# A fused encoder block: the expert loop staged over two blocks, with paired weight rows and a plain fp32 down product

## Chip, cores and metric

One core of a Trainium2 chip. The metric is the device time of the whole kernel in microseconds, lower is better.

## What is computed

One encoder block on x of 1024 tokens by 1024 features, fp32, one sequence. First comes a convolutional mixer behind a norm and a conditioning (projections, two gated convolution branches, an output product). Then a second norm, and a mixture of experts: each token takes two of 32 SwiGLU experts. The tokens of an expert are gathered in blocks of 128 rows. Cut to what matters here:

```python
def expert_block(args):
    xblk, e = args                       # 128 x 1024
    a = xblk @ w_gate[e]                 # 1024 x 512
    u = xblk @ w_up[e]                   # 1024 x 512
    return (jax.nn.silu(a) * u) @ w_down[e]   # 512 x 1024

yb = lax.map(expert_block, (xb, blk_e)).reshape(n_rows, d)
yb = yb * w_buf[:, None]
out = jnp.zeros_like(xt).at[tok_buf].add(yb)
```

The result times a gate row (gt2) is added to x, and a last norm follows. With these inputs 33 blocks hold tokens; a block's empty rows are left out by the gather and the scatter.

## The kernel before

The code is one program with a list of instructions for each engine; order between engines is kept by semaphores, and every engine takes its own list strictly in order. The mixer (up to about 1040 us) and the routing (to about 1082 us) are not touched. There, as in the expert loop, a large product is made of three fp32r matmuls (`three`, lines 1162 to 1166): both operands are split into a high half (a cast, fp32r) and a low half (the operand less its high half), and hi x hi, hi x lo and lo x hi add up in PSUM. The statistics of the mixer (line 1220) use a plain fp32 matmul of the same shape, which the profile records as two.

**Buffers of the expert loop** (lines 214 to 225). A block's weights are six chunks of 128 x 2048 fp32, 1 MB each. Chunks 0 to 3 hold gate and up rows of four groups of 256 input features, chunks 4 and 5 the down rows. Each chunk exists once raw (`e_raw`), once high (`e_hi`) and once low (`e_lo`). The gathered rows `xg`, their transposed halves `xT_hi` and `xT_lo` and the output `y_sb` exist twice.

**SyncE** (lines 396 to 427) loads weights. For block b+1 it waits for each of the four gate/up chunks until VectorE has split block b's (`gu_lo`), issues two transfers of 512 KB (`load_gu`, L400), then for each down chunk until its split is done (`d_lo`), and issues one of 1 MB (`load_down`, L404).

**GpSimd** (lines 524 to 550) gathers the rows of block b+2 (L528) once TensorE has transposed those in that buffer, copies the indices and weights of block b, waits for ScalarE's output, multiplies it by the gate row (L545), scatters it with an add into DRAM (L547) and waits until that has landed.

**ScalarE** (lines 703 to 727), for each block: casts of down chunks 4 and 5 (L710), sigmoid of the first half of the gate columns (L712), cast of chunk 0 of the next block (L691), high half of the first transposed hidden rows (L715), sigmoid of the second half (L717), chunk 1, second hidden half (L720), chunk 2, high half of the next rows (L699), chunk 3, and the output out of PSUM times its weight (L727).

**VectorE** (lines 1129 to 1145) takes the same order for the low halves: L1135 for down chunks, L1104 for gate/up chunks, L1120 for hidden rows, L1108 for rows; L1114 and L1116 multiply gate and up.

**TensorE** (lines 1380 to 1401), for each block: gate/up of the first 256 hidden columns with all eight feature tiles, then of the other 256, down products of chunk 4, transposes of the hidden rows (L1343) and of the next block's rows (L1338), down products of chunk 5. Gate/up of the two halves are 48 matmuls of 512 columns, down 24. Chunk q is free for the next cast when the second half has used it (`gu_used`).

Names and lines that recur: `three` L1164 to L1166, `gate_up` L1346, `down` L1368, `gu_split` on ScalarE L687 and on VectorE L1102, `held` (a wait, L334), `f_o` L1154 in the final norm.

## Time and profile before

| | |
|---|---|
| device time, median of 3 runs | 1873.6 us (1873.36 to 1873.72) |
| span of the profiled execution | 1872.6 us |
| its mean granted TensorE clock | 0.947 |
| TensorE busy, whole kernel | 1619.8 us, 86% |
| VectorE busy | 1380.1 us, 74% |
| ScalarE busy | 808.7 us, 43% |
| GpSimd busy | 359.5 us, 19% |
| packets of SyncE's queue, share of 16 engines | 47.5% |

The page gives a span, from the first to the last instruction, and no separate time for the profiled execution; the median of the runs is 1.0 us above that span. A row of a group of instructions has the line, engine, operation, tiles written and read, shapes and count, then busy us and mean ns of one, then idle time of the engine before them and what ended it. Matmuls overlap, so the mean of one is longer than the distance between starts.

### The profile page before, as it was taken

What the parts mean: (1) busy time and instruction counts of PE and PEld (TensorE: products, weight loads), DVE (VectorE), ACT (ScalarE), POOL (GpSimd) and SP (SyncE); (2) the same over time, 40 slices, a digit from 0 to 9 for tenths busy, and PEclk for the clock granted to TensorE, in tenths of its full rate; (3) what the DMA queues carried; (4) which work ended last, traced back from release to release, by engine and by line L of the source; (5) the groups of instructions that cost most, each with busy time, mean ns of one, the idle gap of its engine ahead of it and who ended that gap; (6) DMA issues with size and microseconds to landing.
All of it is one profiled execution on the core that took longest, in us unless ns stands there. A gap on an engine that the chain in (4) does not pass through costs nothing.

```text
span 1872.6 us, 21983 instructions
## 1 busy us (share of the span) xinstructions
PE 1619.8 (86%) x7040; PEld 1306.4 (70%) x7040; DVE 1380.1 (74%) x1217; ACT 808.7 (43%) x738; POOL 359.5 (19%) x274
## 2 busy tenths in 40 slices
PE   2799999999999979979899568888888888888880
PEld 2688888888888857757688456666666666666660
DVE  5686977868769783483454568888888888888885
ACT  3411111111021122142221257777777777777773
POOL 0100000000000000000000034344444444333441
PEclk9999999999999989989999679999999999999995
DMA  7422313323233244233352468988888888998845
GB/s 259 127 90 86 116 56 123 101 90 106 73 100 113 67 153 143 74 117 119 121 175 90 169 223 308 304 306 307 306 302 304 300 308 307 311 319 304 308 142 193
DMA packets 201362, 352.05 MB, mean 188 GB/s; under 512 B 17228, under 2 KB 90956, under 8 KB 201333
## 3 DMA queue, kind: packets, MB, share of 16 engines
q1 hardware_dynamic: 184630, 309.71, 47.5%
q0 software_dynamic: 16704, 41.98, 7.7%
q8 instruction: 16, 0.26, 0.1%
q14 instruction: 12, 0.10, 0.0%
HBM read 323.84 MB, written 46.66 MB: 198 GB/s over the span
## 4 chain that ended last, share of the span: by engine, by line
PE 48%; DMA 18%; POOL 12%; issue 12%; DVE 7%; ACT 1%; POOLq 1%; SPq 0%; DVEq 0%; ACTq 0%
DMA d_x<-y_sb,s_idx 17%; PE ps L1164 15%; PE ps L1165 15%; PE ps L1166 15%; POOL xg L528 5%; POOL y_sb L545 4%; POOL g_idx L526 2%; PE ps L1220 1%; DVE macc L797 1%; PE ps L1286 1%; POOL s_idx L540 1%; DVE f_o L1154 1%; DVE s L912 1%; DVE conf L903 0%; DMA prow<-in_c_dram 0%
## 5 line engine op out<-in xcount | busy, mean ns | idle before, releaser
L1164 PE MATMUL ps<-A_hi,w_hi 128*128 128x512 f32 x1024 | 402.5, 393 | 23.5 <-DVE A_lo L892 13.0
L1165 PE MATMUL ps<-A_lo,w_hi 128*128 128x512 f32 x1024 | 400.7, 391 | 0.0
L1166 PE MATMUL ps<-A_hi,w_lo 128*128 128x512 f32 x1024 | 400.6, 391 | 0.0
L1104 DVE TENSOR_TENSOR e_lo<-e_raw,e_hi 128x2048 fp32r<-128x2048 f32 x136 | 380.4, 2818 | 1.1 <-issue 1.1
L882 DVE SCALAR_TENSOR_TENSOR conv_acc_b<-glu,colc,conv_acc_b 128x1024 f32<-128x1024 f32 x232 | 298.0, 1285 | 10.5 <-DVE rows L874 1.4
L691 ACT CAST e_hi<-e_raw 128x2048 fp32r<-128x2048 f32 x136 | 259.4, 1910 | 51.5 <-PE ps L1166 51.5
L1164 PE MATMUL ps<-e_hi,xT_hi 128*128 128x512 f32 x528 | 224.8, 426 | 62.1 <-DVE e_lo L1104 59.7
L1164 PEld LDWEIGHTS ps<-A_hi,w_hi 128*128 128x128 f32 x1024 | 193.8, 189 | 65.9 <-issue 17.8
L1165 PEld LDWEIGHTS ps<-A_lo,w_hi 128*128 128x128 f32 x1024 | 193.9, 189 | 40.6 <-issue 0.5
L1166 PEld LDWEIGHTS ps<-A_hi,w_lo 128*128 128x128 f32 x1024 | 193.7, 189 | 40.6
L1165 PE MATMUL ps<-e_lo,xT_hi 128*128 128x512 f32 x528 | 218.1, 413 | 0.0
L1166 PE MATMUL ps<-e_hi,xT_lo 128*128 128x512 f32 x528 | 218.0, 413 | 0.0
L1164 PEld LDWEIGHTS ps<-e_hi,xT_hi 128*128 128x128 f32 x528 | 106.1, 201 | 97.8 <-DVE e_lo L1104 73.2
L1135 DVE TENSOR_TENSOR e_lo<-e_raw,e_hi 128x2048 fp32r<-128x2048 f32 x66 | 147.9, 2279 | 0.0
L577 ACT CAST w_hi<-w_raw 128x1024 fp32r<-128x1024 f32 x72 | 73.6, 1047 | 166.5 <-PE ps L1166 163.4
L1164 PE MATMUL ps<-e_hi,hT_hi 128*128 128x512 f32 x264 | 107.7, 408 | 38.5 <-DVE hT_lo L1120 38.5
L767 DVE TENSOR_TENSOR w_lo<-w_raw,w_hi 128x1024 fp32r<-128x1024 f32 x72 | 88.0, 1223 | 63.0 <-ACT w_hi L577 60.0
L1166 PEld LDWEIGHTS ps<-e_hi,xT_lo 128*128 128x128 f32 x528 | 106.3, 201 | 24.5
L710 ACT CAST e_hi<-e_raw 128x2048 fp32r<-128x2048 f32 x66 | 122.3, 1901 | 0.4
L1165 PEld LDWEIGHTS ps<-e_lo,xT_hi 128*128 128x128 f32 x528 | 106.6, 202 | 21.6
L545 POOL TENSOR_TENSOR y_sb<-y_sb,rows 128x1024 f32<-128x1024 f32 x33 | 82.7, 2507 | 125.2 <-ACT y_sb L727 125.2
L1166 PE MATMUL ps<-e_hi,hT_lo 128*128 128x512 f32 x264 | 104.4, 395 | 0.0
(227 smaller groups left out, 2140.4 us busy)
## 6 DMA issues: line engine op xcount, KB each, us to landing
e_raw<-in_w_gate_dram SPq DMA_DIRECT2D x132, 512.0 KB, 3.8
e_raw<-in_w_up_dram SPq DMA_DIRECT2D x132, 512.0 KB, 4.9
e_raw<-in_w_down_dram SPq DMA_DIRECT2D x66, 1024.0 KB, 8.4
w_raw<-in_w_in_dram SPq DMA_DIRECT2D x56, 512.0 KB, 4.2
stream<-in_w_ada_dram SPq DMA_DIRECT2D x48, 512.0 KB, 5.5
xn<-in_x_dram SPq DMA_DIRECT2D x8, 512.0 KB, 7.2
d_short<-conv_acc_a POOLq DMA_DIRECT2D x8, 512.0 KB, 4.0
d_gate_a<-gate_st POOLq DMA_DIRECT2D x8, 512.0 KB, 2.9
```

Of the source, the lines that this page charges most:

```text
L528: g.indirect_dma_start(xg[:, slot, :], None, d_h2, bass.IndirectOffsetOnAxis(ap=g_idx[:, slot:slot + 1], axis=0), bounds_check=S - 1, oob_ ...
L545: g.tensor_tensor(y_sb[:, s, :], y_sb[:, s, :], rows[:, GT2, :], ALU.mult).then_inc(s_yw, 1)
L577: a.copy(w_hi[:, slot, :], w_raw[:, slot, :]).then_inc(w_hi_done, 1)
L691: a.copy(e_hi[:, q, :], e_raw[:, q, :]).then_inc(gu_hi, 1)
L710: a.copy(e_hi[:, 4 + q, :], e_raw[:, 4 + q, :]).then_inc(d_hi, 1)
L767: v.tensor_tensor(w_lo[:, slot, :], w_raw[:, slot, :], w_hi[:, slot, :].bitcast(F32), ALU.subtract).then_inc(w_lo_done, 1)
L882: lstep(v.scalar_tensor_tensor(conv_acc_b[:], glu[:, t:t + S], w, conv_acc_b[:], ALU.mult, ALU.add))
L1104: v.tensor_tensor(e_lo[:, q, :], e_raw[:, q, :], e_hi[:, q, :].bitcast(F32), ALU.subtract).then_inc(gu_lo, 1)
L1135: v.tensor_tensor(e_lo[:, 4 + q, :], e_raw[:, 4 + q, :], e_hi[:, 4 + q, :].bitcast(F32), ALU.subtract).then_inc(d_lo, 1)
L1164: t.matmul(dst, st_hi, mv_hi, start=first, stop=False)
L1165: t.matmul(dst, st_hi, mv_lo, start=False, stop=False)
L1166: return t.matmul(dst, st_lo, mv_hi, start=False, stop=last)
```

## The change

A block's work is spread over two steps. Step b (lines with `b, par = pair * 2 + (1 + s), 1 - s`) does gate/up of block b and the down product of block b-1; block 0's gate/up stands ahead of the loop and the last down product behind it.

- Gate and up of a block go to one PSUM slot of their own, slots 0 and 1 in turn, and are done in one pass over the chunks. Slot 2 takes row transposes, slot 3 hidden transposes and the down product.
- `load_gu` gives a partition two consecutive rows (4 KB in one piece, before two pieces of 2 KB); the rows' transposes take every second column to match.
- The down product is one plain fp32 matmul in place of three, on raw weights and on hidden rows that are copied once and not split. Splits of chunks 4 and 5 and of the hidden rows go.
- A down chunk's buffer is free when TensorE has used it (`d_used`). SyncE loads gate/up of block b+2 and then down of block b+1.
- The SwiGLU part has one sigmoid and two multiplies of 512 columns.
- VectorE takes the output out of PSUM, times weight and gate row in one instruction; ScalarE's output copy and GpSimd's multiply go. GpSimd scatters it in the next step. The last block has buffers and index of its own.
- One sigmoid of one column is placed ahead of the loop on ScalarE.

```diff
             def load_gu(q, e):
                 for part, w in ((0, w_gate), (1, w_up)):
-                    dst = e_raw[:, q, :].rearrange("p (k w n) -> p k w n", k=2, w=2)[:, :, part, :]
-                    src = w[bass.ds(e, 1), 2 * q * P:2 * (q + 1) * P, :].rearrange("a (k p) n -> p (a k) n", p=P)
+                    dst = e_raw[:, q, part * D:(part + 1) * D].rearrange("p (k n) -> p k n", k=2)
+                    src = w[bass.ds(e, 1), 2 * q * P:2 * (q + 1) * P, :].rearrange("a (p k) n -> p (a k) n", p=P)
                     sp.dma_start(dst, src).then_inc(e_full[q], 16)
...
             with sp.Fori(0, NBLK) as b:
-                with sp.If(b < n_blk):
-                    with sp.If(b + 1 < n_blk):
-                        e_next = sp.value_load(tab[0:1, bass.ds(b + 1, 1)], min_val=0, max_val=NE - 1)
+                with sp.If(b + 1 < n_blk):
+                    with sp.If(b + 2 < n_blk):
+                        e_gu = expert_of(b + 2)
                         for q in range(4):
-                            held(gu_lo, b * 4 + (q + 1))
-                            load_gu(q, e_next)
-                        for q in range(2):
-                            held(d_lo, b * 2 + (q + 1 + CREDIT_DOWN))
-                            load_down(q, e_next)
-
-                    with sp.If(n_blk < b + 2):
+                            held(gu_lo, b * 4 + (4 + q + 1))
+                            load_gu(q, e_gu)
+                    with sp.If(n_blk < b + 3):
                         for q in range(4):
-                            sp.wait_ge(gu_lo, b * 4 + (q + 1))
+                            sp.wait_ge(gu_lo, b * 4 + (4 + q + 1))
                             sp.sem_inc(e_full[q], 32)
+                    e_down = expert_of(b + 1)
+                    for q in range(2):
+                        held(d_used, b * 2 + (q + 1))
+                        load_down(q, e_down)
...
+                        held(t_done, b + 1)
+                        gather(s, b + 2, b * 2 + 2)
+                        g.tensor_copy(s_idx[:, 1 - s:2 - s], idx_all[:, bass.ds(b - 1, 1)]).then_inc(p_copy, 1)
+                        held(p_copy, b * 2 + 3)
+
+                        pool.wait_ge(y_st, b * 16 - 16)
                         pool.sem_inc(y_free, 1)
+                        held(y_ev, b + CREDIT_Y)
+                        scatter(y_sb[:, 1 - s, :], s_idx[:, 1 - s:2 - s])
...
+            def h_hi(value):
+                act.wait_ge(ht_ps, value)
+                a.copy(hT[:].rearrange("p f n -> p (f n)"), ps[:, 3, 0:F]).then_inc(ht_sb, 1)
...
+            def gate(par, value, before):
+
+                act.wait_ge(gu_used, value)
+                if before is not None:
+                    act.wait_ge(a_h, before)
+                a.activation(sg[:], ps[:, par, 0:F], ACT.Sigmoid).then_inc(sgd, 1)
...
+            for q in range(3):
+                gu_split(q, 64, q + 1)
+            gate(0, 4, None)
+            gu_split(3, 64, 4)
             with act.Fori(0, NBLK // 2) as pair:
                 for s in range(2):
-                    with act.If(pair * 2 + s < n_blk):
-                        b = pair * 2 + s
+                    b, par = pair * 2 + (1 + s), 1 - s
+                    with act.If(b < n_blk):
+                        x_hi(1 - par, b + 2)
                         for q in range(2):
-                            act.wait_ge(e_full[4 + q], b * 16 + 16)
-                            act.wait_ge(d_used, b * 2 + (q - 1 + CREDIT_DOWN))
-                            a.copy(e_hi[:, 4 + q, :], e_raw[:, 4 + q, :]).then_inc(d_hi, 1)
-                        act.wait_ge(gu0, b + 1)
-                        a.activation(sg[:, 0, :], ps[:, 0, 0:F // 2], ACT.Sigmoid).then_inc(sgd, 1)
-                        gu_split(0, b * 32 + 64, b * 4 + 1)
-                        act.wait_ge(ht_ps, b * 2 + 1)
-                        a.copy(hT_hi[:, 0:2, :], ps[:, 3, 0:2 * P]).then_inc(ht_hi, 1)
-                        act.wait_ge(gu_used, b * 4 + 4)
-                        a.activation(sg[:, 1, :], ps[:, 0, F:F + F // 2], ACT.Sigmoid).then_inc(sgd, 1)
-                        gu_split(1, b * 32 + 64, b * 4 + 2)
-                        act.wait_ge(ht_ps, b * 2 + 2)
-                        a.copy(hT_hi[:, 2:4, :], ps[:, 3, 4 * P:6 * P]).then_inc(ht_hi, 1)
+                            gu_split(q, b * 32 + 64, b * 4 + (q + 1))
+                        h_hi(b)
                         gu_split(2, b * 32 + 64, b * 4 + 3)
-                        x_hi(1 - s, b + 3)
+                        gate(par, b * 4 + 4, b)
                         gu_split(3, b * 32 + 64, b * 4 + 4)
-                        act.wait_ge(d_used, b * 2 + (2 + CREDIT_DOWN))
-                        act.wait_ge(y_free, b + (CREDIT_STORE - 1))
-                        act.wait_ge(s_w, b + 1)
-                        a.activation(y_sb[:, s, :], ps[:, 2, :], ACT.Copy, scale=w_blk[:, s:s + 1]).then_inc(y_ev, 1)
+            h_hi(n_blk)
...
+            def hidden(par, n):
+
+                dve.wait_ge(sgd, n)
+                v.tensor_tensor(hid[:], ps[:, par, 0:F], sg[:], ALU.mult).then_inc(a_h, 1)
+                dve.wait_ge(a_h, n)
+                v.tensor_tensor(hid[:], ps[:, par, F:2 * F], hid[:], ALU.mult).then_inc(hd, 1)
+
+            def y_out(dst, blk, used):
+
+                dve.wait_ge(d_used, used)
+                v.scalar_tensor_tensor(dst, ps[:, 3, :], w_all[:, bass.ds(blk, 1)], rows[:, GT2, :], ALU.mult, ALU.mult).then_inc(y_ev, 1)
...
+            x_lo(1, 2)
+            for q in range(3):
+                gu_split(q, 4 + q + 1)
+            hidden(0, 1)
+            gu_split(3, 8)
             with dve.Fori(0, NBLK // 2) as pair:
                 for s in range(2):
-                    with dve.If(pair * 2 + s < n_blk):
-                        b = pair * 2 + s
+                    b, par = pair * 2 + (1 + s), 1 - s
+                    with dve.If(b < n_blk):
+                        x_lo(1 - par, b + 2)
                         for q in range(2):
-                            dve.wait_ge(d_hi, b * 2 + (q + 1))
-                            v.tensor_tensor(e_lo[:, 4 + q, :], e_raw[:, 4 + q, :], e_hi[:, 4 + q, :].bitcast(F32),
-                                            ALU.subtract).then_inc(d_lo, 1)
-                        hidden(0, b * 2 + 1, b * 2 + 1, hd0)
-                        h_lo(0, b * 2 + 1)
-                        gu_split(0, b * 4 + 5)
-                        hidden(1, b * 2 + 2, b * 2 + 2, hd1)
-                        gu_split(1, b * 4 + 6)
-                        h_lo(1, b * 2 + 2)
-                        x_lo(1 - s, b + 2)
+                            gu_split(q, b * 4 + (4 + q + 1))
                         gu_split(2, b * 4 + 7)
+                        hidden(par, b + 1)
                         gu_split(3, b * 4 + 8)
+                        dve.wait_ge(y_free, b)
+                        y_out(y_sb[:, 1 - par, :], b - 1, b * 2)
+            y_out(y_last[:], n_blk - 1, n_blk * 2)
...
             def rows_transpose(slot):
                 for k in range(KT):
-                    last = t.transpose(ps[:, 1, k * P:(k + 1) * P], xg[:, slot, k * P:(k + 1) * P], ident[:])
+                    pair_k = xg[:, slot, k // 2 * 2 * P:(k // 2 + 1) * 2 * P].rearrange("t (p w) -> t w p", w=2)
+                    cols_k = pair_k[:, k % 2, :]
+                    last = t.transpose(ps[:, 2, k * P:(k + 1) * P], cols_k, ident[:])
                 last.then_inc(t_done, 1)
 
-            def hidden_transpose(half):
-                for f in range(2):
-                    last = t.transpose(ps[:, 3, half * 4 * P + f * P:half * 4 * P + (f + 1) * P], hid[:, half, f * P:(f + 1) * P], ident[:])
+            def hidden_transpose():
+                for f in range(FT):
...
+            def gate_up(q, par, b):
+
+                pe.wait_ge(gu_lo, b * 4 + (q + 1))
+                for kk in range(2):
+                    k = 2 * q + kk
+                    for part in range(2):
+                        mv = slice(part * D + kk * F, part * D + (kk + 1) * F)
+                        last = three(ps[:, par, part * F:(part + 1) * F], xT_hi[:, par, k * P:(k + 1) * P], xT_lo[:, par, k * P:(k + 1) * P],
+                                     e_hi[:, q, mv], e_lo[:, q, mv], k == 0, k == KT - 1)
+                last.then_inc(gu_used, 1)
+
+            def down(q, value):
+
+                pe.wait_ge(e_full[4 + q], value)
+                for kk in range(2):
+                    f = 2 * q + kk
+                    for h in range(2):
+                        ch_ = slice(kk * D + h * H, kk * D + (h + 1) * H)
+                        last = t.matmul(ps[:, 3, h * H:(h + 1) * H], hT[:, f, :], e_raw[:, 4 + q, ch_], start=(f == 0), stop=(f == FT - 1))
+                last.then_inc(d_used, 1)
+
+            n_blk = pe.value_load(tab[0:1, NBLK:NBLK + 1], min_val=PAIRS // P, max_val=NBLK - 1)
             pe.wait_ge(xg_full[0], 16)
             rows_transpose(0)
+
+            pe.wait_ge(xg_full[1], 16)
+            pe.wait_ge(xTlo, 1)
+            rows_transpose(1)
+            for q in range(4):
+                gate_up(q, 0, 0)
             with pe.Fori(0, NBLK // 2) as pair:
                 for s in range(2):
-                    with pe.If(pair * 2 + s < n_blk):
-                        b = pair * 2 + s
+                    b, par = pair * 2 + (1 + s), 1 - s
+                    with pe.If(b < n_blk):
+                        pe.wait_ge(xg_full[1 - par], pair * 16 + 32)
                         pe.wait_ge(xTlo, b + 1)
-                        pe.wait_ge(hd0, b + 1)
-                        gate_up(0, s, b)
-                        pe.wait_ge(hd1, b + 1)
-                        gate_up(1, s, b)
-                        pe.wait_ge(ht_lo, b * 2 + (1 + CREDIT_DOWN))
-                        pe.wait_ge(d_lo, b * 2 + (1 + CREDIT_DOWN))
-                        pe.wait_ge(y_ev, b + 1)
-                        down(0)
-                        down(1)
-                        pe.wait_ge(hd1, b + 2)
-                        hidden_transpose(1)
-                        pe.wait_ge(xg_full[1 - s], pair * 16 + 16 * (1 + s))
-                        rows_transpose(1 - s)
-                        pe.wait_ge(ht_lo, b * 2 + (2 + CREDIT_DOWN))
-                        pe.wait_ge(d_lo, b * 2 + (2 + CREDIT_DOWN))
-                        down(2)
-                        down(3)
+                        rows_transpose(1 - par)
+                        pe.wait_ge(hd, b - 1 + CREDIT_HID)
+                        for q in range(2):
+                            gate_up(q, par, b)
+                        pe.wait_ge(hd, b + CREDIT_HID)
+                        pe.wait_ge(y_ev, b - 1 + CREDIT_Y)
+                        hidden_transpose()
+                        for q in range(2, 4):
+                            gate_up(q, par, b)
+                        pe.wait_ge(ht_sb, b)
+                        for q in range(2):
+                            down(q, b * 16)
+            pe.wait_ge(hd, n_blk + CREDIT_HID)
+            pe.wait_ge(y_ev, n_blk + (CREDIT_Y - 1))
+            hidden_transpose()
+            pe.wait_ge(ht_sb, n_blk)
+            for q in range(2):
+                down(q, n_blk * 16)
```

## Rows read from the trace of the kernel before

**Rows 1.** Busy time by stretch, 1300 to 1400 us; columns as the first row says.

```profile
core 0: us, PE busy (x) PEld busy (x) DVE busy (x) ACT busy (x) POOL busy (x), PEclk, DMA share, GB/s
1300.00:1400.00 100.00, 87.93 (x384) 69.90 (x384) 83.81 (x61) 74.07 (x64) 40.06 (x27) 0.95 0.87 303
```

**Rows 2.** Who TensorE waited for, blocks 1 to 32 (us in total, times, longest).

```profile
PE ps L1164 <- DVE e_lo L1104: 59.7, 32, 1.9
PE ps L1164 <- DVE hT_lo L1120: 36.2, 31, 1.2
```

**Rows 3.** Instruction groups of sixteen blocks, 1396 to 1750 us, each shape apart.

```profile
L1104 DVE TENSOR_TENSOR e_lo<-e_raw,e_hi 128x2048 fp32r<-128x2048 f32 x64 | 180.1, 2835 | 0.0
L691 ACT CAST e_hi<-e_raw 128x2048 fp32r<-128x2048 f32 x64 | 122.3, 1911 | 24.4 <-PE ps L1166 24.4
...
L1135 DVE TENSOR_TENSOR e_lo<-e_raw,e_hi 128x2048 fp32r<-128x2048 f32 x32 | 71.7, 2279 | 0.0
...
L1108 DVE TENSOR_TENSOR xT_lo<-ps,xT_hi 128x1024 fp32r<-128x1024 f32 x16 | 19.6, 1225 | 18.8 <-ACT xT_hi L699 18.8
...
L699 ACT CAST xT_hi<-ps 128x1024 fp32r<-128x1024 f32 x16 | 16.3, 1018 | 0.0
...
L720 ACT CAST hT_hi<-ps 128x256 fp32r<-128x256 f32 x16 | 6.0, 374 | 13.3 <-PE ps L1343 13.3
```

**Rows 4.** Timeline of one block, TensorE: start us, us, engine, line, operation.

```profile
1404.50 0.39 PE L1164 MATMUL ps<-e_hi,xT_hi 128*128 128x512 f32 x1
...
1408.35 0.39 PE L1166 MATMUL ps<-e_hi,xT_lo 128*128 128x512 f32 x1
...
1420.85 1.04 PE L1338 MATMUL ps<-ident,xg 128*128 128x128 f32 x8
```

**Rows 5.** TensorE by shape: the plain fp32 matmul of the statistics, whole kernel.

```profile
L1220 PE MATMUL ps<-conf,mean_w 128*128 128x512 f32 x32 | 13.9, 592 | 0.0
```

**Rows 6.** Timeline of SyncE's transfer issues in one block.

```profile
1410.81 0.37 SPq L400 DMA_DIRECT2D e_raw<-in_w_gate_dram  x1
1411.28 0.42 SPq L400 DMA_DIRECT2D e_raw<-in_w_up_dram  x1
1412.94 2.56 SPq L404 DMA_DIRECT2D e_raw<-in_w_down_dram  x2
```

**Rows 7.** SyncE's load of an expert number (L416): duration, first and last start.

```profile
L416 SPq SEQ_ASSERT  x2: 18/18/18, 1417.0 to 1438.4; - x2
```

**Rows 8.** Transfers: down loads (L404) to landing; issue table of the page.

```profile
DMA to landing us min/median/max: 5.7/8.4/17.4
...
e_raw<-in_w_gate_dram SPq DMA_DIRECT2D x132, 512.0 KB, 3.8
e_raw<-in_w_up_dram SPq DMA_DIRECT2D x132, 512.0 KB, 4.9
```

**Rows 9.** Transfers in 1038 to 1040, 1050 to 1056 and 1398.94 to 1752.9 us.

```profile
DMA packets 416, 0.82 MB, mean 410 GB/s; under 512 B 16, under 2 KB 16, under 8 KB 416
...
DMA packets 859, 2.48 MB, mean 413 GB/s; under 512 B 55, under 2 KB 55, under 8 KB 858
...
DMA packets 47950, 109.00 MB, mean 308 GB/s; under 512 B 4961, under 2 KB 4961, under 8 KB 47950
...
q0 software_dynamic: 4608, 8.99, 10.5%
```

**Rows 10.** Timeline of the first block.

```profile
1088.26 1.97 PE L1338 MATMUL ps<-ident,xg 128*128 128x128 f32 x8 [8.84 <-DMA xg<-d_h,g_idx]
...
1092.67 0.79 PE L1164 MATMUL ps<-e_hi,xT_hi 128*128 128x512 f32 x1 [2.44 <-DVE xT_lo L1108]
...
1101.10 0.38 ACT L712 ACTIVATE sg<-ps 128x256 f32<-128x256 f32 x1 [3.51 <-PE ps L1166]
```

**Rows 11.** Timeline of the last block.

```profile
1827.92 1.11 ACT L727 ACTIVATE y_sb<-ps,w_blk 128x1024 f32<-128x1024 f32 x1 [0.20 <-PE ps L1166]
```

**Rows 12.** Chain that ended last, its end.

```profile
1832.46 5.77 DMA d_x<-y_sb,s_idx
```

134 lines of the change are left out of this document (56 added, 78 removed).

## The prediction

> **What bounds the kernel now.** I read the busy time by stretch first. In the expert loop, VectorE is busy 84 of 100 us, TensorE 88, the transfer engines 87 [rows 1]: nobody is full, so something alternates. The waits say what: in 32 blocks TensorE waits 59.7 us for L1104 (the low half of a gate/up chunk) and 36.2 us for L1120 (the low half of the hidden rows), 3.0 us a block [rows 2]. One block's splits can only begin when the block before has used its chunks, and its down product is too short a cover. The chain that ended last runs through GpSimd's scatters, but GpSimd sits idle before each and only its last scatter sets the end [rows 12]. Sixteen blocks take 354 us [rows 3], 22.1 each.
>
> **The change, part by part.** I call step i the time T(i) to T(i+1) in which TensorE transposes rows of block i+1, does gate/up of block i, and at the end the down product of block i-1. There are 33 blocks, steps 1 to 32, with block 0's gate/up ahead and the last down product behind.
>
> *TensorE.* Gate/up keeps 48 matmuls: 17 starts apart take 3.85 us, so 0.228 us each [rows 4], 10.95 us. The down product loses 24 matmuls of 0.23 (5.5 us) and gets 8 plain fp32 ones. The statistics show that kind: 16 in code, 32 in the profile, 13.9 us, 0.868 us each [rows 5], so 6.95 us, dearer by 1.4. Twelve transposes at 0.13 (eight in 1.04 [rows 4]) are 1.55, and hand-overs I put at 0.2. Sum **19.65 us** if nothing makes it wait; both old waits go, since a chunk's split now has a period less 2.7 us to be ready and costs 1.91 + 2.28 [rows 3]. Transposes with a stride of two words are not in the trace: nothing lost, or double, 1.0 us; I take nothing, as the columns are as many. It lies before the point that I find decisive below.
>
> *VectorE* loses two splits of 2.28, 4.6 us, and the low halves of the hidden rows. L1104 and L1135 are one shape with means of 2835 and 2279 ns [rows 3]; the difference lies in the split beside GpSimd's multiply, which goes too, 4 x 0.56 = 2.2 us. It gains the weighted output, near L1108's 1.23 (1024 columns out of PSUM), say 1.3. From about 18.6 (84% of 22.1) to 13 us a block: no bound. *ScalarE* loses two casts of 1.91 and the output copy; its new cast of 512 hidden columns lies between 0.37 (256) and 1.02 (1024) [rows 3], 0.6. The table load I price at nothing either way: it can run while ScalarE waits. *GpSimd* loses the multiply; its scatter now goes out about 2.5 us into the next step and its gather of two blocks ahead behind that, over ten us before it is needed, so that move costs nothing.
>
> *SyncE's queue is what I think ends last.* Its order is written out: gate/up of block b+2, then down of b+1, and each down load waits for the down *product* of block b, no longer for the split. That product's second half ends at T(b+2). Behind that wait, in the same queue, stand all gate/up loads of block b+3, whose buffers had been free for long. So at T(i) SyncE issues down part 1 and then gate/up chunks 0 to 3 of block i+1, which are wanted in this same step. ScalarE's order is also written out: split chunk 0, split chunk 1, then the hidden copy of block i-1, for which the down product of this step waits. So the loop is: end of a down product, three chunks of 1 MB landed, a split, the hidden copy, the next down product.
> - SyncE wakes 0.2 us after.
> - First chunk, issue to landing: gate 3.8, up 4.9 and issued 0.47 later [rows 6, 8], so 5.4; a down load at best 5.7 [rows 8]. I take 5.5.
> - Two more behind it, at a full queue's rate: 1.049 MB at 413 GB/s is 2.54 us [rows 9], 5.1. Paired rows halve the pieces; filled with 2 KB pieces the queue moved 410, with 4 KB pieces 413 GB/s [rows 9], so this is worth nothing here. SyncE is ready for the next load 1.5 us after an issue [rows 6, 7], less than a chunk.
> - The gather and scatter queue took 10.5% of 354 us in 16 blocks, 2.3 us a block [rows 9]. None or all can fall within these three chunks. The scatter's data start late in them and the gather's after them; I take 0.7.
>
> Chunk 1 is there 0.2 + 5.5 + 5.1 + 0.7 = 11.5 us after T(i). Add 0.1, the split 1.91, the copy 0.6, 0.15 of signals, and 6.95 of down product: **21.2 us**, more than 19.65, so steps 2 to 31 take this. With the ends 0 and 2.3 of the last term it is 20.5 to 22.8.
>
> What the rule would make of it: the Trainium skill (DMA: Bandwidth & Descriptors, Specifications) gives a core about 358 GB/s from HBM; by that a chunk is 2.93 us and the step 22.4. Here the trace disagrees, with 413 GB/s over 6 us; its stage mean of 308 is one of a queue with gaps.
>
> *Start.* Block 0's first gate/up matmul is at 1092.67. Ahead of it now comes a second set of transposes, 1.97 us, the clock granted then being half. Its first 24 matmuls took until about 1100.9, the other 24 take 5.5, so T(1) is 1108.3 [rows 10]. Step 1 has its weights already: T(2) = 1128.0. Thirty steps of 21.2 make 1764.0. Step 32 loads no weights for a next block, 19.65: 1783.6.
> *End.* Output of block 31 1.5, transposes and signals 0.9, copy 0.6 and 0.2, down 6.95, output 1.7, scatter 5.8 [rows 12]: 17.65, which gives 1801.3. Before, the last scatter landed at 1832.46 + 5.77 = 1838.2 [rows 12], behind the last output that ScalarE took from PSUM at 1827.92 [rows 11]. What follows is untouched. So the span goes from 1872.6 to 1835.7, 36.9 us less. The profiled execution's span stands 1.0 us under the median of the runs, 1873.6, which I take as what lies around it: **1837 us**.
>
> **Rivals.**
> *TensorE becomes the bound.* If chunk 1 lands within 9.95 us of T(i), the product never waits: 30 x 1.55 = 46.5 us less, 1790 us. For it: all engines have room, and the transfers of a block, 6.3 MB at 413 GB/s plus 2.3, are 17.5 us. Against: three chunks in line need 10.8 with nothing else in the way.
> *Slow chunks, by the page's rule.* If weights come at some 13% under the burst rate while everything runs, three chunks cost 1.2 us more, the step is 22.4 and the gain is used up: 1872 us, no change. For it: 308 GB/s over sixteen blocks; against: both bursts in rows 9. The rule is the one on a core's share of HBM in the Trainium skill's DMA page.
> *Slower: the same loop at the stage's mean rate.* Place: the queue wait before gate/up. If a chunk needs 1.049 MB at 308 GB/s, 3.4 us, the three are 2.6 dearer, of which 0.7 was counted: a step of 23.1 to 23.3, 1897 us. It turns slower from a landing of chunk 1 later than 12.7 us. For it: a down load takes 8.4 us in the median today, against 5.7 at best [rows 8]. Against: at T(i) the queue is nearly empty, as the load ahead was issued half a product, 3.5 us, earlier.
> *The change does less than it says.* Table loads remain or strided transposes double: both fall in the step's first 12 us, where the product waits anyway, so 1837 to 1845.
>
> **How the numbers follow.** My forecast has 0.58, TensorE as the bound 0.18, slow chunks 0.08, the slower loop 0.12, the incomplete change 0.04. A measurement of this kernel tells a difference from about 0.2%, 3.7 us. Faster by that: 0.58 + 0.18 + 0.04 = 0.80; within: most of the slow chunks, 0.07; slower: 0.13. The range takes in TensorE as the bound with a little below it, and the slow chunks: 1788 to 1876; the slower loop is what is left out. The forecast's own range is 1816 to 1870: its lower end has no gather or scatter among the three chunks, its upper end nearly all of both.
>
> **What would show it.** No wait on e_lo before gate/up; a wait of about 1.5 us a step before the first plain down matmul, released by ScalarE's hidden copy; ahead of that, ScalarE idle until a gate/up chunk lands; SyncE held by TensorE's down product, then a burst of nine loads; starts of steps 21.2 us apart; VectorE near 13 us busy a step, TensorE's down matmuls 0.87 us each. If the steps are 19.7 us apart and SyncE issues gate/up before T(i), I have misread the order. If ScalarE's casts lie back to back before the hidden copy, the bound is another. If gate/up chunks land more than 12.7 us after the product's end, the kernel is slower.

## Result, and the profile after

The changed kernel takes **1976.9 us** (median of 4 runs, 1973.2 to 1980.1) against 1873.6 before (4 runs, same chip): 1.0556 times as long, 95% interval 1.0539 to 1.0572. The prediction said 1837. The profiled execution took 1973.2 us and has a span of 1971.4; the sums below are made against it.

The page of the kernel after, busy time, chain by engine and by line, and transfer issues (count, size, us to landing):

```profile
span 1971.4 us, 20777 instructions
...
PE 1695.6 (86%) x6776; PEld 1265.2 (64%) x6776; DVE 1180.8 (60%) x1053; ACT 560.1 (28%) x508; POOL 150.6 (8%) x208
...
PE 63%; DMA 17%; DVE 7%; ACT 5%; SPq 4%; issue 3%; POOL 0%; DVEq 0%; ACTq 0%; POOLq 0%
PE ps L1394 16%; DMA e_raw<-in_w_up_dram 15%; PE ps L1194 14%; PE ps L1196 14%; PE ps L1195 14%; ACT e_hi L716 3%; SPq L403 2%; PE ps L1250 1%; DVE macc L825 1%; ACT hT L724 1%; SPq L410 1%; SPq L407 1%; PE ps L1316 1%; DVE f_o L1184 1%; DVE s L940 0%
...
e_raw<-in_w_gate_dram SPq DMA_DIRECT2D x132, 512.0 KB, 8.5
e_raw<-in_w_up_dram SPq DMA_DIRECT2D x132, 512.0 KB, 10.7
```

VectorE lost 199 us of work, ScalarE 249, GpSimd 209, and the kernel got slower. The chain no longer runs through GpSimd but through L1394, the plain down product, and through up loads, whose way from issue to landing grew from 4.9 us to 10.7 [rows 8].

Busy time by stretch of the kernel after, the stretch of [rows 1] and 1300 to 1700 us:

```profile
1300.00:1400.00 100.00, 83.09 (x299) 55.04 (x298) 46.95 (x29) 34.60 (x26) 12.28 (x16) 0.91 0.73 266
...
1300.00:1700.00 400.00, 334.61 (x1166) 217.28 (x1165) 196.89 (x123) 145.02 (x106) 46.17 (x61) 0.89 0.71 258
```

Every engine is idler than before; TensorE is less busy and its granted clock is lower (0.91 against 0.95). The waits in 1300 to 1700 us (us in total, times, longest), the last line that of SyncE's queue:

```profile
ACT e_hi L716 <- DMA e_raw<-in_w_up_dram: 156.3, 37, 7.1
...
PE ps L1394 <- ACT hT L724: 65.4, 15, 4.8
...
SPq L338 <- PE ps L1394: 286.9, 32, 16.1
```

The old waits of [rows 2] are gone. TensorE waits 4.4 us a step for the hidden copy, ScalarE over 10 us a step for chunks, and SyncE stands 287 of 400 us behind the down product. One step in the timeline (us at start, duration, engine, line; in brackets the idle time ahead and who ended it), put together from the answers for each engine:

```profile
1399.15 10.18 PE L1394 MATMUL ps<-e_raw,hT 128*128 128x512 f32 x16 [4.53 <-ACT hT L724]
...
1406.13 3.83 SPq L407 DMA_DIRECT2D e_raw<-in_w_down_dram  x2
...
1409.17 1.11 PE L1368 MATMUL ps<-ident,xg 128*128 128x128 f32 x8
...
1411.58 0.35 SPq L403 DMA_DIRECT2D e_raw<-in_w_gate_dram  x1
...
1411.64 1.61 POOL L542 DMA_INDIRECT d_x<-y_sb,s_idx  x1 [23.13 <-DVE y_sb L1149]
...
1415.68 0.43 SPq L403 DMA_DIRECT2D e_raw<-in_w_up_dram  x1
...
1418.05 1.91 ACT L716 CAST e_hi<-e_raw 128x2048 fp32r<-128x2048 f32 x1 [6.72 <-DMA e_raw<-in_w_up_dram]
...
1423.81 1.90 ACT L716 CAST e_hi<-e_raw 128x2048 fp32r<-128x2048 f32 x1 [3.84 <-DMA e_raw<-in_w_up_dram]
1425.61 0.58 ACT L724 COPY hT<-ps 128x512 f32<-128x512 f32 x1
...
1426.32 8.55 PE L1394 MATMUL ps<-e_raw,hT 128*128 128x512 f32 x16 [4.63 <-ACT hT L724]
```

This is the loop of the prediction: product ends (1409.2), second down load ends its issue (1409.96), eight gate/up issues in a burst, chunk 0 cast at 1418.05, chunk 1 at 1423.81, hidden copy, next product. Two of its pieces are longer. **Chunk 1** is cast 5.76 us behind chunk 0, where the prediction has 2.54 + 0.7. And **the product** takes 8.55 to 10.18 us in the two steps shown, where it has 6.95. The clock in the first product above, by stretch (the last three columns are granted clock, share of transfer engines, GB/s):

```profile
1399.00:1405.00 6.00, 5.85 (x7) 2.52 (x8) 5.38 (x5) 4.31 (x4) 0.00 (x0) 0.50 0.17 68
1406.00:1409.00 3.00, 3.00 (x8) 1.34 (x7) 1.26 (x1) 0.00 (x0) 0.00 (x0) 1.00 0.58 171
```

After 4.53 us without work TensorE is granted half its clock, 1.2 GHz, and gets 2.4 GHz back only inside the product. The Trainium skill (TensorE: Matmul & The Clock Gate, Part 1) says that an idle engine's clock falls to one half; these rows agree, with 0.50.

Means over steps 3 to 30, in us from the end of the down product before, worked out from the starts in the timeline (a step goes from product end to product end):

| | chunk 0 cast | chunk 1 cast | product starts | product takes | step |
|---|---|---|---|---|---|
| predicted | 8.3 | 11.6 | 14.25 | 6.95 | 21.2 |
| after | 8.35 | 14.09 | 16.61 | 9.41 | 26.02 |
| e_copy_first | | | ahead of the chunks | | 19.2 to 21.4 |
| e_order | 3.71 | 6.43 | 12.17 | 7.03 | 19.20 |
| e_warm | 8.60 | 13.70 | 16.84 | 7.07 | 23.91 |
| e_noscatter | 8.42 | 11.18 | 13.70 | 7.43 | 21.13 |
| e_late_scatter | 9.19 | 11.75 | 14.27 | 7.92 | 22.18 |
| e_early_gather | 8.70 | 14.12 | 16.64 | 9.33 | 25.97 |
| e_spread | 8.28 | 13.09 | 15.61 | 9.02 | 24.62 |
| e_unpaired | 8.66 | 14.58 | 17.10 | 9.62 | 26.71 |

(What these kernels are follows. The trace of e_late_scatter is of a slow execution, 1860.6 us against 1824.1 to 1831.3 of its other four, with steps 14 to 25 at 23 to 24 us and the others near 21, so its row is too long: in its steps 3 to 12 chunk 1 is cast at 11.19 us.)

### The profile page after: what moved, and what is told of

Read it like the earlier page. It is cut to its first block, busy times and chain, and to the rows that moved or that the text cites. A ratio compares the mean times of both kernels' runs of the same rounds, so it can differ in the third digit from the quotient of the medians.

```text
span 1971.4 us, 20777 instructions
## 1 busy us (share of the span) xinstructions
PE 1695.6 (86%) x6776; PEld 1265.2 (64%) x6776; DVE 1180.8 (60%) x1053; ACT 560.1 (28%) x508; POOL 150.6 (8%) x208
## 4 chain that ended last, share of the span: by engine, by line
PE 63%; DMA 17%; DVE 7%; ACT 5%; SPq 4%; issue 3%; POOL 0%; DVEq 0%; ACTq 0%; POOLq 0%
PE ps L1394 16%; DMA e_raw<-in_w_up_dram 15%; PE ps L1194 14%; PE ps L1196 14%; PE ps L1195 14%; ACT e_hi L716 3%; SPq L403 2%; PE ps L1250 1%; DVE macc L825 1%; ACT hT L724 1%; SPq L410 1%; SPq L407 1%; PE ps L1316 1%; DVE f_o L1184 1%; DVE s L940 0%
## 5 line engine op out<-in xcount | busy, mean ns | idle before, releaser
L1133 DVE TENSOR_TENSOR e_lo<-e_raw,e_hi 128x2048 fp32r<-128x2048 f32 x136 | 311.1, 2289 | 330.9 <-ACT e_hi L716 329.9
L1394 PE MATMUL ps<-e_raw,hT 128*128 128x512 f32 x528 | 306.4, 746 | 126.9 <-ACT hT L724 126.9
L716 ACT CAST e_hi<-e_raw 128x2048 fp32r<-128x2048 f32 x136 | 258.3, 1902 | 320.8 <-DMA e_raw<-in_w_up_dram 309.0
L1394 PEld LDWEIGHTS ps<-e_raw,hT 128*128 128x128 f32 x528 | 124.6, 243 | 294.8 <-issue 294.7
L1194 PE MATMUL ps<-e_hi,xT_hi 128*128 128x512 f32 x528 | 212.4, 402 | 0.0
L1196 PE MATMUL ps<-e_hi,xT_lo 128*128 128x512 f32 x528 | 206.7, 392 | 0.0
L1195 PE MATMUL ps<-e_lo,xT_hi 128*128 128x512 f32 x528 | 206.2, 391 | 0.0
L542 POOL DMA_INDIRECT d_x<-y_sb,s_idx x32 | 51.5, 1609 | 703.4 <-DVE y_sb L1149 679.8
L720 ACT CAST xT_hi<-ps 128x1024 fp32r<-128x1024 f32 x34 | 34.5, 1015 | 213.1 <-PE ps L1368 213.1
L1149 DVE SCALAR_TENSOR_TENSOR y_sb<-ps,w_all,rows 128x1024 f32<-128x1024 f32 x32 | 41.1, 1284 | 55.1 <-PE ps L1394 55.1
## 6 DMA issues: line engine op xcount, KB each, us to landing
e_raw<-in_w_up_dram SPq DMA_DIRECT2D x132, 512.0 KB, 10.7
```

The source lines that it names most:

```text
L542: g.indirect_dma_start(d_x1, bass.IndirectOffsetOnAxis(ap=idx_ap, axis=0), rows_ap, None, bounds_check=S - 1, oob_is_err=False, compute_op ...
L716: a.copy(e_hi[:, q, :], e_raw[:, q, :]).then_inc(gu_hi, 1)
L1133: v.tensor_tensor(e_lo[:, q, :], e_raw[:, q, :], e_hi[:, q, :].bitcast(F32), ALU.subtract).then_inc(gu_lo, 1)
L1149: v.scalar_tensor_tensor(dst, ps[:, 3, :], w_all[:, bass.ds(blk, 1)], rows[:, GT2, :], ALU.mult, ALU.mult).then_inc(y_ev, 1)
L1194: t.matmul(dst, st_hi, mv_hi, start=first, stop=False)
L1195: t.matmul(dst, st_hi, mv_lo, start=False, stop=False)
```

## Experiments

All are edits of the changed kernel unless said otherwise. Ratios are to the kernel before, on the same chip.

**1. Is it the loop through SyncE's written order? (e_order, e_copy_first, e_both.)** In e_order SyncE issues gate/up loads one block earlier, so that they stand ahead of the wait for the down product:

```diff
+            e_two = sp.value_load(tab[0:1, 2:3], min_val=0, max_val=NE - 1)
+            for q in range(4):
+                sp.wait_ge(gu_lo, 4 + q + 1)
+                load_gu(q, e_two)
             with sp.Fori(0, NBLK) as b:
...
-                        e_gu = expert_of(b + 2)
+                        e_gu = expert_of(b + 3)
                         for q in range(4):
-                            held(gu_lo, b * 4 + (4 + q + 1))
+                            held(gu_lo, b * 4 + (8 + q + 1))
```

e_copy_first leaves the loads and cuts the loop on ScalarE:

```diff
                         x_hi(1 - par, b + 2)
+                        h_hi(b)
                         for q in range(2):
                             gu_split(q, b * 32 + 64, b * 4 + (q + 1))
-                        h_hi(b)
```

> SyncE issues the gate/up loads one step earlier, ahead of its wait for the down product; everything else is as in the changed kernel. Theory A (the loop over SyncE's order: end of product, gate/up chunk 1 landed after 14.5 us, split, hidden copy, next product): the loop is open, TensorE waits for nothing, a step takes 19.7 us in place of 26.6 and the kernel about 1795 us (1785 to 1815). Rival B (the plain product on raw weights itself costs 9 to 10 us, whatever the wait ahead of it): the wait goes but the product stays, steps of 22 to 23 us, 1860 to 1890. Rival C (the transfers of 4 KB pieces are too slow for the loop in any order): steps stay above 25 us, over 1930.

> ScalarE does the hidden copy before it splits gate/up chunks 0 and 1; SyncE's late loads stay. Theory A: the product no longer waits for a landing, the wait ahead of it goes from 4.6 us to near nothing, and the late chunks are just in time for the next gate/up: steps of 19.7 to 21.5 us, 1790 to 1850. Rival B: product stays at 9 to 10 us, 1860 to 1890. Rival C: gate/up waits for its chunks instead, steps above 25 us, over 1930.

> Both edits together. Theory A: TensorE is already the bound with the order alone, so within 5 us of that run. If it is over 10 us faster, a second wait on ScalarE's order was left in that run.

Measured: e_order **1771.4 us**, ratio 0.9461 [0.9445, 0.9477]; e_copy_first 1779.9, 0.9498 [0.9482, 0.9513]; e_both 1781.8, 0.9522 [0.9504, 0.9540]. Moving one group of loads, or one copy of 0.58 us, turns 5.6% slower into about 5% faster: the loop is what ended last, and cutting it at either place is enough. Both came out faster than the ranges of theory A (1785 to 1815 and 1790 to 1850), as a step without waits takes 19.20 us and not the 19.7 that I had put. e_order, 1300 to 1700 us, busy time and its one large group of the down product (busy, mean ns, idle before):

```profile
1300.00:1700.00 400.00, 400.00 (x1583) 279.03 (x1582) 269.14 (x167) 201.57 (x147) 100.84 (x84) 1.00 0.96 349
...
L1398 PE MATMUL ps<-e_raw,hT 128*128 128x512 f32 x333 | 146.4, 592 | 0.0
```

TensorE is busy all 400 us at full clock and waits for nothing. Its step is 19.20 us, the prediction's floor of 19.65. What missed is e_both, which should have been within 5 us of e_order and took 10 more. The casts of both chunks now stand behind the hidden copy and start at 7.36 and 9.17 us, not 3.71 and 6.43. SyncE, which waits for the splits of these chunks, then issues the two down loads 2.3 and 3.3 us after the product's end in place of 0.5 and 1.2, and TensorE waits for them. Its waits, same stretch:

```profile
PEld ps L1398 <- DMA e_raw<-in_w_down_dram: 13.3, 22, 1.8
```

**2. The clock (e_warm).** Twenty matmuls whose result nobody reads fill TensorE's wait:

```diff
+                        for _w in range(20):
+                            t.matmul(ps[:, 1 - par, 0:H], xT_hi[:, par, 0:P], xT_hi[:, par, 0:H], start=True, stop=True)
                         pe.wait_ge(ht_sb, b)
```

> Changed kernel, with 20 extra fp32r matmuls of 512 columns (20 x 0.228 = 4.6 us) into an unused PSUM slot just where TensorE waits for the hidden copy. They compute nothing that is used. If the down product's 8.5 to 10.2 us is a matter of the granted clock, which is at half when it starts after the wait: clock stays full, the product takes 7 us, steps are 2.4 us shorter (24.2 us), about 1900 us in spite of the added work. If the clock is not the cause: no gain, 1975 us or more.

Measured: 1918.7 us, 1.0241 [1.0224, 1.0259]: 58 us less than the changed kernel, with 640 matmuls more. I had expected about 1900, so the gain is some 20 us smaller than forecast, while the product's time is as forecast. Timeline of e_warm, the filler (L1422) and the product:

```profile
1407.58 4.70 PE L1422 MATMUL ps<-xT_hi 128*128 128x512 f32 x20
1412.12 7.03 PE L1394 MATMUL ps<-e_raw,hT 128*128 128x512 f32 x16
```

The product takes 7.03 us, which is the prediction's 8 x 0.868 = 6.95. Chunk 1 is still late, at 13.70. So 2.34 of the product's 9.41 us are the half clock, and the rest of the step's loss is not.

**3. What makes chunk 1 late? (e_hold, e_noscatter, then e_late_scatter, e_early_gather.)** Theory D was that chunks 2 and 3, issued in the same burst, share the transfer engines with chunk 1; theory E that the scatter does. e_hold makes SyncE wait for the cast of chunk 1 ahead of chunk 2:

```diff
                         for q in range(4):
                             held(gu_lo, b * 4 + (4 + q + 1))
+                            if q == 2:
+                                held(gu_hi, b * 4 + (8 + 2))
                             load_gu(q, e_gu)
```

e_noscatter gives the scatter an index out of range for all blocks but the first and the last, so it leaves out the experts' results of the others:

```diff
-                        g.tensor_copy(s_idx[:, 1 - s:2 - s], idx_all[:, bass.ds(b - 1, 1)]).then_inc(p_copy, 1)
+                        g.tensor_copy(s_idx[:, 1 - s:2 - s], idx_all[:, NBLK:NBLK + 1]).then_inc(p_copy, 1)
```

> Changed kernel; SyncE issues gate/up chunks 2 and 3 only after ScalarE has split chunk 1 of the same block. In the changed kernel chunk 1 lands 14.5 us after the product's end, not the 11.5 of my sum. Theory D (chunks 2 and 3, issued within 4 us of it, share the engines with chunk 1, since a later transfer does not wait for an earlier one to be complete): chunk 1 lands at 11.5 to 12.5, the wait ahead of the product shrinks from 4.6 to about 2 us, the product gets back its full clock, steps of 22 to 23.5 us, 1830 to 1890. Rival E (the queue is strictly in order and chunk 1 is late for another reason, such as the gather and scatter): chunk 1 lands as late as before, 1970 or more.

> Changed kernel; the scatters of all but the first and last block get indices outside the tensor, so they move no rows: the experts' results of these blocks are left out. Rival E (GpSimd's transfers hold up chunk 1): it lands 1.5 to 3 us earlier, 1880 to 1930. Theory D: the scatter moves about a quarter of a chunk, at most 1 us earlier, 1940 to 1975.

Measured: e_hold 1867.9 us, 0.9973 [0.9962, 0.9985] (median of ten runs; one took 7805 us, which I can't explain, and without it the median is 1867.0); e_noscatter 1831.1, 0.9767 [0.9741, 0.9792]. e_hold brings chunk 1 to 12.0 us, which looked like theory D, but its trace shows that the scatter moved too, from 2.3 us behind the product's end to 7.2, so it separates nothing. e_noscatter has the burst whole and chunk 1 at 11.18. Its time lies 49 us under the range of theory E (1880 to 1930). Chunk 1's 2.9 us in thirty steps are 87 us; the rest came by way of the clock, as the product behind the shorter wait takes 7.43 us and not 9.41. Two instructions of its ScalarE, timeline:

```profile
1406.95 1.91 ACT L716 CAST e_hi<-e_raw 128x2048 fp32r<-128x2048 f32 x1 [6.37 <-DMA e_raw<-in_w_up_dram]
1409.77 1.91 ACT L716 CAST e_hi<-e_raw 128x2048 fp32r<-128x2048 f32 x1 [0.91 <-DMA e_raw<-in_w_up_dram]
```

They are 2.82 us apart, close to the 2.54 of a full queue. To separate the two with all work done, e_late_scatter gathers one step earlier and holds the scatter until chunk 1 is cast; e_early_gather has the gather's move alone:

```diff
-                        held(t_done, b + 1)
-                        gather(s, b + 2, b * 2 + 2)
+                        held(t_done, b + 2)
+                        gather(1 - s, b + 3, b * 2 + 3)
...
                         held(y_ev, b + CREDIT_Y)
+                        held(s_ch1, b + 1)
                         scatter(y_sb[:, 1 - s, :], s_idx[:, 1 - s:2 - s])
```

> Changed kernel with all its work; GpSimd issues the gather of a block one step earlier, ahead of its wait for the output, and holds each scatter until gate/up chunk 1 of the running step has landed. Leaving the scatter out let chunk 1 land at 11.2 us where the changed kernel has 14.1; holding chunks 2 and 3 gave 12.0, but it also moved the scatter from 2.3 to 7.3 us after the product's end. Theory E (the scatter's traffic is what delays chunk 1): chunk 1 at 11 to 11.7, steps of 20.5 to 21.5 us, 1810 to 1840. Theory D (it is the later loads, and the scatter matters only by its bytes): chunk 1 stays at 13 or later, over 1930.

> Control for the late scatter: the gather one step earlier, the scatter where it was. Theory E: the scatter still meets chunks 0 and 1, so chunk 1 lands at 13.5 to 14.5 and the time is within 20 us of 1977. If this alone gives more than 50 us, the gather was the trouble and not the scatter.

Measured: 1828.9 us, 0.9761 [0.9741, 0.9781], and 1971.5, 1.0530 [1.0512, 1.0547]. Theory E holds, and D falls as the cause: with the later loads in the burst as before, moving the scatter from 2.3 to 12.7 us behind the product's end gives back 143 us, as much as leaving it out; chunk 1 at 11.19 and the time are in theory E's ranges. The control says less of the gather than I had meant it to: GpSimd takes its list in order, so in e_early_gather the gather, though one block ahead, still goes out behind the scatter, at 4.99 us (4.98 before), and in e_late_scatter the held scatter moves it to 16.9. What shows that it is the scatter is e_noscatter, where the gather goes out at 5.9 us and chunk 1 is on time.

**4. Why does 1.8 us of transfer work delay a chunk by 2.9? (e_spread.)** In the changed kernel queue q0, gather and scatter, took 7.3% of 400 us with 16 scatters: 1.8 us a step for both. Yet with the scatter chunk 1 is 2.9 us later (14.09 against 11.18 in e_noscatter; in steps 3 to 12 14.05 against 11.19 in e_late_scatter). Theory F: a block's rows fill its first partitions, so the live rows load some of the 16 transfer engines and leave others idle, and a chunk is there only when its last part is. e_spread numbers the rows of a block so that 0 to 63 go to even partitions and the rest to odd ones:

```diff
             step(v.scalar_tensor_tensor(rowf[:], blkf[:], -float(P), posf[:], ALU.mult, ALU.add))
+            step(v.tensor_scalar(posf[:], rowf[:], float(P // 2), -float(P - 1), ALU.is_ge, ALU.mult))
+            step(v.scalar_tensor_tensor(rowf[:], rowf[:], 2.0, posf[:], ALU.mult, ALU.add))
```

> Changed kernel; the rows of a block are numbered so that they fill every second partition first (row r goes to 2r, or 2r - 127 from 64 on), at two small VectorE instructions ahead of the loop. All work is done. Leaving out the scatter let chunk 1 land 2.9 us earlier, more than the scatter's mean share of all 16 engines, about 1.5 us. Theory F (a block holds 62 rows of 128 in the mean, in its first partitions, so its gather and scatter load only some of the transfer engines, and a chunk lands when the slowest engine is done): spread out, the scatter delays chunk 1 by about half, 12.3 to 13.2 us, steps of 22.5 to 24.5, 1850 to 1930. Rival G (the delay is the scatter's total work or its order in the queues): no change, 1965 to 1985.

Measured: 1931.1 us, 1.0316 [1.0298, 1.0333], 46 less than the changed kernel; chunk 1 at 13.09. The same bytes in the same order, placed otherwise, come 1.0 us earlier. That is what theory F asks for in the chunk's time; the step (24.62 us) and the kernel's time lie just outside its ranges. It is part of the delay, not all of it. The packets in the traces say which part. Means over steps 3 to 30, from the end of the down product to the landing of chunk 1 (0.1 us before its cast):

| | us | moved by SyncE's queue | summed time of q0's packets, by 16 engines |
|---|---|---|---|
| after | 13.97 | 4.48 MB | 2.02 us |
| e_spread | 12.95 | 4.07 MB | 2.02 us |
| e_noscatter | 11.02 | 4.03 MB | 0.35 us |

In the changed kernel 0.45 MB more of weights had moved when chunk 1 was complete than without the scatter: other loads of the burst had got ahead of it. At the 406 GB/s that this queue moves in e_noscatter from 6 to 9 us this is 1.1 us. With the rows spread, all but 0.04 MB of it is gone. The other 1.8 us of the delay is in both kernels, close to the additional time of q0's packets, 2.02 less 0.35. The load of each single transfer engine is not in the trace, so F is supported and not seen.

**5. Parts of the change alone (e_unpaired, e_order_unpaired, e_plain_only).** The unpaired kernels load 2 KB pieces and transpose neighbouring columns, as before. e_plain_only is the kernel *before* with only the plain down product; a down chunk is then free when TensorE has used it:

```diff
-                            held(d_lo, b * 2 + (q + 1 + CREDIT_DOWN))
+                            held(d_used, b * 2 + (q + 1 + CREDIT_DOWN))
```

> Changed kernel with the paired rows undone: gate/up loads in pieces of 2 KB again and transposes of consecutive columns. By my sum the pieces are worth nothing (410 against 413 GB/s): within 10 us of 1977. If 4 KB pieces matter to a landing (84 to 94 ns for 2 KB against 159 for 4 KB, 6 to 15%), the three chunks take 0.5 to 1.2 us more and the kernel is 15 to 40 us slower. If the stride of two words cost the transposes anything it falls ahead of the product's wait and hides.

> The version with gate/up loads issued a step earlier, with 2 KB pieces and consecutive columns. TensorE is the bound at 19.2 us and the transfers have room: within 3 us of 1771. In the changed kernel the same undoing cost 16 us, which by theory A came by way of the landings. If the strided transposes cost anything, this run is faster than 1771 by 32 times it.

> Kernel before with one part of the change alone: the down product is a plain fp32 matmul on raw weights and unsplit hidden rows, so a down chunk is held until its product is done, and no two-block staging. TensorE has 1.4 us more of matmuls a block and 1 to 2 us less of waits, so by work alone about 1865 to 1890. Theory A says more: SyncE's wait for the product stands ahead of the next block's gate/up loads here too, and where these come late it costs on top: 1890 to 1960. Rival: 1850 or less, then the plain product alone is a gain and the staging loses it.

Measured: e_unpaired 1992.7 us, 1.0652 [1.0634, 1.0670]; e_order_unpaired 1773.7, 0.9469 [0.9453, 0.9484]; e_plain_only 1910.7, 1.0205 [1.0188, 1.0222]. Pairing is worth 16 us where chunk 1 ends last (it lands 0.5 us earlier) and nothing where TensorE does. The plain product alone costs 37 us in the old order. That is in the range of theory A (1890 to 1960), but the trace does not bear the theory out here. SyncE does stand behind TensorE, as its waits in 1300 to 1700 us show, to be held against 216.5 us for L1104 and 46.8 for L1135 in the kernel before:

```profile
SPq L334 <- PE ps L1357: 253.2, 34, 11.3
```

Yet the gate/up loads still come in time: of the idle time before ScalarE's casts of their chunks, 1.6 us in 400 is a wait for a load.

```profile
L691 ACT CAST e_hi<-e_raw 128x2048 fp32r<-128x2048 f32 x69 | 131.3, 1903 | 31.6 <-PE ps L1151 29.9 <-DMA e_raw<-in_w_up_dram 1.6
```

What a block costs more is TensorE's own work. Its busy time goes from 19.3 to 21.1 us a block, most of it the product (two halves of 3.60 us where the three matmuls take 5.5), and its idle time from 3.0 to 2.4. Together that is the 1.2 us by which a block is longer (23.45 us against 22.28). My 1865 to 1890 by work alone had put 1.4 us more for the product and 1 to 2 us less of waits, of which 0.6 came.

**6. Is the plain product worth having? (e_three, e_three_first, e_three_spread.)** e_three is e_order with the three-matmul down product and its splits. e_three_first also puts the down loads ahead of the gate/up loads in SyncE's step:

```diff
                 with sp.If(b + 1 < n_blk):
+                    e_down = expert_of(b + 1)
+                    for q in range(2):
+                        held(d_lo, b * 2 + (q + 2))
+                        load_down(q, e_down)
                     with sp.If(b + 3 < n_blk):
...
-                    e_down = expert_of(b + 1)
-                    for q in range(2):
-                        held(d_lo, b * 2 + (q + 2))
-                        load_down(q, e_down)
```

e_three_spread adds the row order of e_spread to that.

> The version with gate/up loads issued a step earlier, and the plain fp32 product undone: the down product is three fp32r matmuls on split chunks and split hidden rows again. TensorE loses 1.4 us a step (19.2 to 17.8), VectorE gains 4.6 + 0.7 on 13 and is the bound at 18.3 to 18.6: 1742 to 1755 us. If VectorE's written order leaves TensorE waiting for the low halves, 1771 or more, and the plain product pays even where TensorE is the bound.

> The three-matmul down product again (2042 us with the down loads behind the next gate/up loads in SyncE's order, ScalarE waiting 13.5 us a step for a down chunk), now with the down loads ahead of them. By theory A that wait was once more SyncE's order: it goes, VectorE is the bound at 18.3 to 19 us a step, 1740 to 1770. If TensorE still waits for low halves: 1775 or more, and the plain product pays.

> The three-matmul version with down loads first, with rows spread over all partitions. There a step takes 17.95 us at first and 18.5 to 19.5 later, with the transfer engines 96% busy. Theory F: spreading takes the unevenness out, so more steps stay at 17.95: 1735 to 1758. Rival G (it is the transfers' total that binds): within 4 us of 1765.

Measured: e_three **2041.6 us**, 1.0906 [1.0884, 1.0927], a miss by some 290 us; e_three_first 1764.9, 0.9438 [0.9422, 0.9453]; e_three_spread **1743.6**, 0.9310 [0.9298, 0.9323], the best of all. In e_three I had built the same fault again: its down loads stand behind gate/up loads that wait for a split late in the step. Its waits, 1300 to 1700 us:

```profile
ACT e_hi L737 <- DMA e_raw<-in_w_down_dram: 216.2, 30, 14.0
...
PE ps L1222 <- DVE hT_lo L1168: 104.7, 15, 9.4
```

ScalarE waits over 14 us a step for a down chunk. With the two groups swapped this is gone, and 277 us with it. Busy time of 1300 to 1600 us, first e_three_first, where chunks are at times late,

```profile
1300.00:1600.00 300.00, 286.03 (x1325) 232.98 (x1325) 275.42 (x175) 209.03 (x142) 93.89 (x62) 1.00 0.98 360
```

then e_three_spread:

```profile
1300.00:1600.00 300.00, 300.00 (x1406) 247.60 (x1405) 292.81 (x185) 223.58 (x151) 98.48 (x65) 1.00 1.02 382
```

TensorE, VectorE (98%) and the transfer engines are all full; its step is 17.93 us. Three fp32r matmuls beat one plain fp32 one (5.5 us against 7.03 a block) once no transfer is late: with packed rows e_three_first and e_order are the same within their intervals (0.9438 and 0.9461), with spread rows it is 28 us ahead of e_order. Spread rows with the plain product in e_order's order were not run; TensorE was busy there in all of 400 us, so I expect little of them. Spreading the rows is worth 21 us here too.

## Why the prediction was wrong

The mechanism was the right one, and its sign wrong, because two terms of the loop were too small. By its own steps:

- **The sum.** T(2) was 1123.5 us (predicted 1128.0): -4.5. Thirty steps took 778.8 us (T(32) is 1902.3), 25.96 each, in place of 636: +142.8. Step 32 took 19.4 (19.65): -0.3. From T(33) to the last scatter's landing 20.5 us (17.65): +2.9. Behind it 29.2 us, where the kernel before has 34.4: -5.2. Together +135.7, the difference of the spans (1971.4 and 1835.7).
- **TensorE's floor**: right. The plain product is 7.03 us at full clock (6.95); with e_order the whole step is 19.20 (19.65); strided transposes cost next to nothing (1.11 us for eight, 1.04 before [rows 4]; e_order_unpaired is no faster). The 0.228 us of a gate/up matmul should have been 0.2265 (3.85 over 17), which is 0.08 us of a step. What was missing is the clock. The working prices the product at full speed right behind a wait that it itself forecasts, although it had used the half clock for the first transposes. **Failed term: "6.95 of down product"**, measured 9.41, +2.46 a step; e_warm, with the wait filled, has 7.07.
- **SyncE's queue** is what ended last, as said. Chunk 0 was cast at 8.35, and 0.2 + 5.5 + 2.54 gives 8.2. The order is right; that the figure is so close is in part luck. The down load ahead of it lands 4.8 us after its issue, not 5.5, and chunk 0 over 3 us behind that, not 2.54: in e_noscatter, where no scatter is in the way, they land at 5.14 and 8.26 us. **Failed term: "The scatter's data start late in them and the gather's after them; I take 0.7"**, together with its upper end of 2.3 from q0's share. From chunk 0 to 1 went 5.74 us, 3.2 over a chunk's own 2.54, so even the upper end is too low. The scatter was issued 2.3 us after T(i) and landed at 12.0, beside chunk 1 (e_late_scatter and e_noscatter show that it is what delays it). By that chunk's landing q0's packets had taken 2.0 us of all 16 engines, near the upper end, and other loads had got 0.45 MB ahead, 1.1 us, for which the sum has no term; with spread rows that part goes.
- The two terms feed each other: the later chunk 1, the longer the wait, and the longer the product: it starts at 13.70, 15.61, 16.61 and 17.10 us in e_noscatter, e_spread, the changed kernel and e_unpaired and takes 7.43, 9.02, 9.41 and 9.62. The start is 2.36 us late and the product 2.46 longer, which is the step's +4.8. In e_noscatter, where chunk 1 comes at 11.18, the step is 21.13 us, the forecast's 21.2.
- **VectorE** at 13 us a step: 49% of 26.0 is 12.8 (196.9 of 400 us), right. **Table load, copy, output**: no wait of theirs ends anything.
- **Start and end.** The last product took 10.07 us, not 6.95, again with a start at half clock. The tail is shorter because SyncE reads the sum back at once (1942.28), where before it did so 5.2 us after the landing (1838.2 and 1843.45); "what follows is untouched" was wrong by that.
- **Rivals.** "Slower: the same loop at the stage's mean rate" had the sign, the place and the condition (chunk 1 later than 12.7 us; it was 14.1), but the wrong price (1897 us) and reason: chunk 0 was on time, and without the scatter chunk 1 came 2.76 us behind it, not 3.4. "Slow chunks, by the page's rule": the Trainium skill (DMA: Bandwidth & Descriptors, Specifications) has about 358 GB/s a core; e_three_spread moved 382 GB/s over 300 us, so the measurement disagrees here, and the cause lay elsewhere. "TensorE becomes the bound" (1790) is what e_order is, at 1771, with chunk 1 at 6.43 us.
- **Pairing** was priced at nothing. That was wrong by 16 us in this kernel and right in e_order.
- The largest omission stands before all terms: having found that loads with free buffers wait behind a product, the prediction still called the change faster, for 0.9 us between a step of 21.2 and one of 22.1. Both things that it had left out or put low (what a wait does to the clock, what collides with a burst) lengthened that loop.

Open: whether the loads that get ahead do so on engines without live rows, as theory F says; what the gather alone does to chunk 1; what e_hold says of chunks 2 and 3; its run of 7805 us.

## What to carry to other kernels

When a change makes a buffer free later, look in the issuing engine's list for what stands *behind* that wait: here loads whose buffers had long been free, and moving them, or the one copy that closed the loop, was worth over 190 us. Price such a loop with all that collides with its burst, and take a queue's mean share as the least that it can cost the chunk beside it: here 1.8 us of share made 2.9 us of delay. Price a TensorE product behind a wait of some microseconds with a start at half clock as well: here 2.3 us on top of 7.0, behind 4.5 us of wait. Then check the repaired order for the next group that stands behind a late wait; e_three had one and lost 277 us to it.

## What the hardware showed that I had not expected

- A scatter of one block (q0: 1.8 us a step with the gather) made the chunk beside it 2.9 us late, and placing its rows on alternate partitions took 1.0 us off that, 46 us of the kernel. Its 4 KB packets take 327 ns each where those of a load take 159 (packets of q0 and of SyncE's queue in the kernel after, 1300 to 1700 us; in e_noscatter the 327 ns packets are gone).
- Work without use made the kernel faster: 20 filler matmuls a step, 4.7 us, took 58 us off (1976.9 to 1918.7).
- Short waits can bring the half clock too: the last down product stands behind waits of 1.98 and 0.76 us with 0.63 us of transposes between them, and it was granted half clock for its first six microseconds. Timeline of the kernel after, then its clock in 1925 to 1931 us:

```profile
1923.65 0.63 PE L1373 MATMUL ps<-ident,hid 128*128 128x128 f32 x4 [1.98 <-DVE y_sb L1149]
1925.03 10.07 PE L1394 MATMUL ps<-e_raw,hT 128*128 128x512 f32 x16 [0.76 <-ACT hT L724]
```

```profile
1925.10:1927.00 1.90, 1.90 (x3) 0.87 (x4) 0.00 (x0) 0.00 (x0) 0.48 (x1) 0.50 0.94 250
1927.00:1931.00 4.00, 4.00 (x6) 1.58 (x5) 0.00 (x0) 0.00 (x0) 0.18 (x1) 0.50 0.29 54
```

- The same transfer engines at a share of 0.98 to 1.02 moved 360 GB/s with rows packed and 382 with rows spread.
